# Inverting the chunk matrices of a linear recurrence on 32x32 blocks instead of 64x64

## The reference

```python
def _wkv7_step(state, inp):
    r_t, w_t, k_t, v_t, a_t, b_t = inp
    sa = jnp.einsum('bhvk,bhk->bhv', state, a_t)
    state = (state * w_t[:, :, None, :] + sa[..., None] * b_t[:, :, None, :]
             + v_t[..., None] * k_t[:, :, None, :])
    y = jnp.einsum('bhvk,bhk->bhv', state, r_t)
    return state, y
```

## Time and profile before

| | us |
|---|---|
| median of 3 runs (3816.68 to 3824.45) | 3817.28 |
| profiled execution, its own time | 3821.82 |
| span of the profile (first to last instruction) | 3820.0 |
| the chunk stage within it | 2341.4 to 2565.1 |

### The profile page before, as it was taken

The page is one execution under the profiler, slowest core; times in us unless marked ns, Lnnn a source line. Parts: engine busy times, 40 slices in busy tenths (PEclk is TensorE's granted clock), DMA queues, the critical chain, the costliest instruction groups (busy, mean ns, idle before and its releaser), DMA issues. The chain is left out here.

```text
span 3820.0 us, 58799 instructions
## 1 busy us (share of the span) xinstructions
PE 3543.2 (93%) x22333; PEld 2862.8 (75%) x22333; DVE 2333.9 (61%) x3638; ACT 1484.4 (39%) x2447; POOL 1348.4 (35%) x831
## 2 busy tenths in 40 slices
PE   8999998989988999899998998885999977889998
PEld 4787866779988999788886346873888854678887
DVE  5713176407998887788888665447566135755642
ACT  3212265325537994333332332222255203424540
POOL 3724300526784335442221001314344511413443
PEclk9999998999999999999999999997899987698999
DMA  7624401535678889999997243112233253033331
GB/s 281 218 91 135 144 36 74 190 107 186 223 234 299 320 321 381 354 366 361 355 352 256 75 138 111 59 42 98 70 94 99 100 143 75 1 127 84 88 121 55
DMA packets 372422, 655.35 MB, mean 172 GB/s; under 512 B 24152, under 2 KB 231896, under 8 KB 369028
## 3 DMA queue, kind: packets, MB, share of 16 engines
q1 hardware_dynamic: 324908, 477.04, 38.5%
q0 software_dynamic: 36864, 134.23, 9.4%
q10 hardware_dynamic: 10456, 41.40, 2.8%
HBM read 554.53 MB, written 98.06 MB: 171 GB/s over the span
## 5 line engine op out<-in xcount | busy, mean ns | idle before, releaser
L96 PE MATMUL ex_hb<-wb_x_hi,ex_uh 128*128 128x384 f32 x1024 | 350.9, 343 | 22.2 <-POOL ex_ul L1676 22.2
L2336 POOL TENSOR_TENSOR pf_wl<-pf_raw,pf_wh 128x2048 fp32r<-128x2048 f32 x48 | 221.3, 4611 | 395.2 <-ACT pf_wh L2283 395.2
L97 PE MATMUL ex_hb<-wb_x_lo,ex_uh 128*128 128x384 f32 x1024 | 344.9, 337 | 0.0
L98 PE MATMUL ex_hb<-wb_x_hi,ex_ul 128*128 128x384 f32 x1024 | 344.7, 337 | 0.0
L96 PE MATMUL es_ob<-es_vh,es_ah 128*128 128x512 f32 x768 | 300.3, 391 | 11.2 <-DVE es_al L2045 11.1
L96 PE MATMUL pf_acc<-wb_x_hi,pf_wh 128*128 128x512 f32 (+2 forms) x768 | 302.6, 394 | 4.7 <-DVE wb_x_lo L2378 4.7
L97 PE MATMUL pf_acc<-wb_x_lo,pf_wh 128*128 128x512 f32 (+2 forms) x768 | 302.1, 393 | 0.0
L98 PE MATMUL pf_acc<-wb_x_hi,pf_wl 128*128 128x512 f32 (+2 forms) x768 | 302.0, 393 | 0.0
L97 PE MATMUL es_ob<-es_vl,es_ah 128*128 128x512 f32 x768 | 299.9, 390 | 0.0
L98 PE MATMUL es_ob<-es_vh,es_al 128*128 128x512 f32 x768 | 299.7, 390 | 0.0
L2024 POOL DMA_INDIRECT es_near<-in_peer_v,wb_picked x128 | 165.9, 1296 | 338.2 <-DVE wb_po L2048 332.4
(11 more groups left out here) (520 smaller groups left out, 8939.7 us busy)
## 6 DMA issues: line engine op xcount, KB each, us to landing
ex_u<-in_uT SPq DMA_DIRECT2D x128, 512.0 KB
es_v<-in_peer_v SPq DMA_DIRECT2D x31, 2048.0 KB
pf_raw<-in_w_up SPq DMA_DIRECT2D x88, 512.0 KB, 5.2
ip_raw<-in_w_in SPq DMA_DIRECT2D x112, 256.0 KB, 4.3
scratch_act<-ex_ge SPq DMA_DIRECT2D x128, 192.0 KB
scratch_G<-eg_gates ACTq DMA_DIRECT2D x12, 2048.0 KB
es_ge<-scratch_act SPq DMA_DIRECT2D x31, 768.0 KB
es_g<-scratch_G SPq DMA_DIRECT2D x31, 768.0 KB
```

Of the source, the lines that this page charges most:

```text
L96: pe.matmul(out, left[0], right[0], start=start, stop=False)
L97: pe.matmul(out, left[0], right[1], start=False, stop=False)
L98: return pe.matmul(out, left[1], right[0], start=False, stop=stop)
L2336: pool.tensor_tensor(wl[:, u], raw[:, u], wh[:, u].bitcast(F32), ALU.subtract).then_inc(w_lo, 1)
```

## The change

- `LEVELS` is 4. The four levels work on 32x32 blocks alone: the tiles `em`, `ws`, `xx` have 32 columns instead of 64, and partition quarters 0 to 31, 32 to 63, 64 to 95, 96 to 127 hold the two diagonal blocks of both heads. `w_of` has 32 matmuls of 32x32 per unit and level, `d_of` has 64.
- The diagonal blocks are first copied together by four ScalarE activations per unit (`pick`, from `ba` to `ub`); GpSimd masks `ub`.
- `l_of` computes only diagonal blocks, with 32 matmuls instead of 16.
- The last level (joining 32 to 64) is a stage of its own for the one off-diagonal block: `last_w` 16 matmuls, `copy_last` (two ScalarE copies), `last_d` 16 matmuls, `corner` (two VectorE copies); `join` on GpSimd spreads the diagonal blocks into the 64x64 tile `xt`, which `az_of` reads.
- `copy_az` moves from VectorE to ScalarE. `copy_v`, `copy_k` and `mv_of` with its copy move to levels 0, 1 and 2.
- The masks loaded are `blocks` and `halves` instead of `lmask` and `emask`.

```diff
-    LEVELS = 5
+    LEVELS = 4
+    RB_ = RC // 2
+        em = sb("rc_em", [P, 2, LEVELS, NC_, RB_])
+        ub = sb("rc_ub", [P, 2, NC_, RB_])
+        xt = sb("rc_xt", [P, 2, NC_, 2, RB_])
+        quarters = [slice(RB_ * g, RB_ * g + RB_) for g in range(4)]
...
                         for c, p in TILES:
                             h, own = heads[c], tok[2 * i + p]
-                            mm = pe.matmul(pp[heads[p], u, 2 + c, i * RC:(i + 1) * RC], ar(s)[h, 0, own], bk(s)[h, 0, own],
-                                           start=True, stop=True)
+                            for j in range(2):
+                                block = slice(own.start + RB_ * j, own.start + RB_ * (j + 1))
+                                mm = pe.matmul(pp[quarters[2 * p + j], u, 2 + c, i * RB_:(i + 1) * RB_], ar(s)[h, 0, block],
+                                               bk(s)[h, 0, block], start=True, stop=True)
...
-                    for c, e in narrow:
-                        h = heads[c]
-                        mm = pe.matmul(one(u, 0)[h, e], em[h, u, lv, e, :], xx[h, u, 0, e, :], start=True, stop=True)
+                    for f in range(NC_):
+                        for g in quarters:
+                            mm = pe.matmul(low(u)[g, f], em[g, u, lv, f, :], xx[g, u, 0, f, :], start=True, stop=True)
...
+                    for f in range(NC_):
+                        for g in quarters:
+                            pe.matmul(pair(u)[g, 0, f], xx[g, u, 1, f, :], ws[g, u, f, :], start=True, stop=True)
+                        for g in quarters:
+                            mm = pe.matmul(pair(u)[g, 1, f], ws[g, u, f, :], xx[g, u, 1, f, :], start=True, stop=True)
...
+                def last_w(n):
+                    u = n % 2
+                    pe.wait_ge(x_added, nth(n, LEVELS - 1))
+                    for f in range(NC_):
+                        for p in range(2):
+                            g = quarters[2 * p]
+                            mm = pe.matmul(low(u)[quarters[2 * p + 1], f], ba[g, n % SLOTS, f, 0, RB_:RC], xx[g, u, 0, f, :],
+                                           start=True, stop=True)
...
+                def last_d(n):
+                    u = n % 2
+                    pe.wait_ge(last_w_copied, 2 * n + 2)
+                    for f in range(NC_):
+                        for p in range(2):
+                            g = quarters[2 * p + 1]
+                            mm = pe.matmul(pair(u)[quarters[2 * p], 1, f], ws[g, u, f, :], xx[g, u, 1, f, :],
+                                           start=True, stop=True)
...
+                    last_w(n)
+                    last_w(n + 1)
+                    last_d(n)
+                    last_d(n + 1)
                     az_of(n)
                     az_of(n + 1)
...
+                def corner(n):
+                    u = n % 2
+                    dve.wait_ge(last_d_done, n + 1)
+                    dve.wait_ge(joined, n + 1)
+                    for p in range(2):
+                        g = quarters[2 * p]
+                        dve.tensor_copy(xt[g, u, :, 1, :], pair(u)[g, 1]).then_inc(xt_full, 1)
...
+                def pick(n):
+                    act.wait_ge(ba_masked, n + 1)
+                    for g in range(4):
+                        act.activation(ub[quarters[g], n % 2], ba[quarters[g], n % SLOTS, :, 0, g % 2 * RB_:(g % 2 + 1) * RB_],
+                                       ACT.Copy).then_inc(picked, 1)
```

More of the change, by code:

```diff
@@ L2503, in _ @@
                         load(i + 1, u)
-                for to, name in zip(masks, ("mask2", "lmask", "emask", "eye2", "ident")):
+                for to, name in zip(masks, ("mask2", "blocks", "halves", "eye2", "ident")):
                     sp.dma_start(to[:], d[name]).then_inc(masks_loaded, 16)
@@ L2855, in d_of @@
                         pe.wait_ge(xt_ready, n + 1)
-                        pe.wait_ge(k_copied, n + 1)
-                        pe.wait_ge(v_copied, n + 1)
+                        pe.wait_ge(ab_copied, 2 * n + 2)
                     pe.wait_ge(w_copied, nth(n, lv))
[L2859 to L2869, removed]
@@ L2877, in mv_of @@
                         h = heads[c]
-                        mm = pe.matmul(one(u, 1)[h, e], ka[h, n % SLOTS, e, 0, :], rows[h, u, V_, e, :], start=True, stop=True)
+                        mm = pe.matmul(one(u, 2)[h, e], ka[h, n % SLOTS, e, 0, :], rows[h, u, V_, e, :], start=True, stop=True)
                     mm.then_inc(mv_done, 1)
@@ L2983, in add @@
                     dve.wait_ge(d_done, nth(n, lv))
[L2984 to L2994, removed]
+                    dve.tensor_tensor(xx[:, u], xx[:, u], pair(u), ALU.add).then_inc(x_added, 1)
+                def corner(n):
[5 more added lines that the diff above has]
+                        dve.tensor_copy(xt[g, u, :, 1, :], pair(u)[g, 1]).then_inc(xt_full, 1)
                 def add_r(n):
@@ L3025, in _ @@
                         add(n + 1, lv)
-                    copy_az(n)
-                    copy_az(n + 1)
+                    corner(n)
+                    corner(n + 1)
                     if n + 2 < KD:
@@ L3088, in _ @@
                         if lv == 0:
+                            copy_v(n)
+                            copy_v(n + 1)
+                        elif lv == 1:
+                            copy_k(n)
+                            copy_k(n + 1)
+                        elif lv == 2:
                             copy_mv(n)
                             copy_mv(n + 1)
+                    copy_last(n)
+                    copy_last(n + 1)
+                    copy_az(n)
+                    copy_az(n + 1)
+                    if n + 2 < KD:
+                        pick(n + 2)
                     copy_y(n)
+                    if n + 2 < KD:
+                        pick(n + 3)
                     copy_y(n + 1)
@@ L3759, in join @@
         return ((s // (2 * m) == t // (2 * m)) & (s // m < t // m)).astype(f)
-    c["lmask"] = np.stack([join(1, t, s), join(1, s, t)], 1)
-    c["emask"] = np.stack([join(m, s, t) for m in (2, 4, 8, 16, 32)], 1)
+    r, t = np.arange(P)[:, None] % (RC // 2), np.arange(RC // 2)[None]
+    c["blocks"] = np.stack([join(1, t, r), join(1, r, t), (r == t).astype(f)] + [join(m, r, t) for m in (2, 4, 8, 16)], 1)
+    first = (np.arange(P) % RC < RC // 2).astype(f)
+    c["halves"] = np.stack([first, 1 - first], 1)
     dist = np.maximum(T - 1 - np.arange(640), 0)
```

88 lines of the change are left out of this document (58 added, 30 removed).

## The result

The changed kernel takes 3903.28 us (median of 4 runs, 3898.56 to 3905.76); the kernel before took 3818.11 beside it (3816.68 to 3824.45). The ratio is 1.0219, with 95% interval 1.0203 to 1.0235. It is 2.2% slower.

What follows compares the result with a forecast made beforehand. Bound after the change: TensorE's program arriving, 256 instructions per 3.65 us. Stage 281.1 + 8 + 2.8 + 6.8 = 298.7 us, 75.0 over 223.7; 3821.8 + 75.0 = 3896.8, less 4.5 to the median: 3892, range 3860 to 3922.

Steps and rivals of the forecast that it cites:

- Number of pieces: TensorE's program in the stage: 19712 instructions after the change, 77 pieces of 256, against 51 before.
- Time per piece: TensorE's program in the stage: 256 instructions arrive in 3.65 us, all 77 in 281.1; a pair's level takes 11.0.
- Start: First 256 instructions of the stage: 2.8 us over a piece, because of the masks between them; stays.
- Loads: Three pieces of program disturbed by loads of the next units took 6.8 us more; this stays.
- What does not fit under a piece: `az_of` and the transposes: work exceeds the program's arrival by some 1 us, twice per pair, 8 us in all.
- Rival (b): Granted clock low through the levels: `az_of`, transposes and others take 36 us more at most, 3928; beyond 3920, chance 0.13.
- The price of a 32x32 matmul: Small matmuls in the levels: 14 ns per record, hidden under the program's arrival, term 0; at 28 ns about 0 to 10 us.
- Copies, additions, masks: Level work on ScalarE, VectorE and GpSimd: copy 0.39 us, addition 0.69, masks half of 1.31; hidden, saving nothing.
- Rival (a): Program no bound in the levels, smaller matmuls pay: 4.0 us per level, 40 us saved in all, 3777; chance 0.06.
- never shows: TensorE's instruction room, four times the others' (128 KB against 32 KB), was said never to show in the stage's 13056 instructions.

Runs made afterwards that it cites:

- the loop: Changed kernel with each pair's four levels as one loop on TensorE instead of written out, one mask buffer instead of four: 3811.5 us, ratio 0.9976 against the kernel before.

## Why the prediction came out right

The forecast was 3892 us and the median is 3903.28, within the range of 3860 to 3922, by the mechanism that was named. The forecast of the stage was 10.4 us too low, and so was that of the time (11.3). Its terms, one by one, for the stage of 309.1 us where 298.7 were expected:

- **Number of pieces.** 77 from the count of matmuls, 77 packets measured. Exact, and so is what the experiments removed: 77 - 36 = 41 in the loop, 77 - 24 = 53 with half the matmuls.
- **Time per piece.** From the resume at 2357.68 to that at 2379.80 lie six pieces in 22.12 us, 3.69 each, which is also the mean of all 42 single pieces without a load beside them; 3.65 was taken from four stretches before. 77 of them: 283.9 against 281.1. The level: 11.54 against 11.0.
- **Start.** The 2.8 us stayed nearly as they were: the first 128 matmul records now take 6.06 us. But the reason given, the masks between them, was wrong. TensorE did not wait there; it was busy from end to end at a low clock, as this stretch of the kernel before shows. The first 64 records of it took 3.69 us; the same 64 of a later pair, at a granted clock of 1.00, took 2.12.

```profile
2341.44:2347.78 6.34, 6.34 (x129) 6.20 (x133) 3.34 (x3) 0.00 (x0) 2.57 (x3) 0.55 0.94 311
```

- **Loads.** Three pieces beside loads took 6.21 + 5.90 + 6.66 us, a fourth 4.63; less 4 x 3.69 that is 8.6, against 6.8.
- **What does not fit under a piece.** The remainder, 309.1 - 283.9 - 2.8 - 8.6 = 13.8 us, against 8: the mis-sized term. `az_of` took 4.76 us for 62 records against 3.60, at a granted clock of 0.75, because it comes while the clock is still low. Over the four pairs it was busy for 21.9 us (first line, changed kernel) against 14.8 (second, before), and for 14.8 in the looped kernel too, where the levels run at the full clock:

```profile
L2917 PE MATMUL rc_pp<-rc_rhs,rc_xt 64*64 64x128 f32 x256 | 21.9, 349 | 0.3
...
L2887 PE MATMUL rc_pp<-rc_rhs,rc_xx 64*64 64x128 f32 x256 | 14.8, 271 | 0.0
```

  That is 7.1 us more, enough for the 5.8 missing. The remainder itself can be found in the trace: eight stretches of two to four pieces without a wait of over 0.5 us, most of them behind an inverse or at the start of a pair, took 91.5 us for 21 pieces, 14.0 more than 3.69 each. How the 14.0 divide between `az_of`, the transposes and the rest was not traced.

**Rival (b), the clock, was half right.** The clock did fall to 0.50, 1.2 GHz, in the levels, where TensorE stands nearly half of each piece. But it cost only what is in the last term, 5.8 us more than forecast and not the 36 of the rival: the work of a piece of 32x32 matmuls ends in under 2.5 us even so, as the stretches show, and the rest is waiting. The loop shows the reverse: where TensorE hardly stands, the granted clock is 1.00 (2369.5 to 2373.6 us, 3.73 us busy of 4.10).

**The price of a 32x32 matmul.** I took 14 ns and said that anything to 28 would not matter. At a clock of 0.50 it is (1.07 - 0.24) / 61 = 13.6 ns from the 62 records shown at 2365.17. In the loop at full clock 128 records of `w_of` took 1.44 us, some 10 ns each. The term was 0 as stated, since 128 records at 13.6 ns are 1.7 us. The 14 ns were read from a row at the full clock, so that they came true at half of it is luck; the bound of 28 ns is what carried the term.

**Copies, additions, masks.** Estimated from halves of known sizes; the groups of the stage:

```profile
L3164 POOL TENSOR_TENSOR rc_em<-rc_ub,rc_blocks 128x256 f32<-128x256 f32 x32 | 22.4, 728 | 313.0 <-ACT rc_ub L3078 313.0
L3020 DVE TENSOR_TENSOR rc_xx<-rc_xx,rc_pp 128x512 f32<-128x512 f32 x32 | 22.0, 688 | 172.9 <-PE rc_pp L2879 172.9
...
L3078 ACT ACTIVATE rc_ub<-rc_ba 32x256 f32<-32x256 f32 x32 | 13.3, 414 | 16.0 <-DVE rc_ba L2994 15.3
...
L3103 ACT ACTIVATE rc_ws<-rc_pp 128x256 f32<-128x256 f32 x32 | 12.3, 384 | 115.1 <-PE rc_pp L2866 115.1
...
L3085 ACT ACTIVATE rc_az<-rc_pp 128x1024 f32<-128x1024 f32 x8 | 8.2, 1024 | 23.7 <-PE rc_pp L2917 23.7
```

The copy was put at 0.39 us and takes 0.384, the addition at 0.69 and takes 0.688, `copy_az` at 1.04 and takes 1.02, a mask at half of 1.31 and takes 0.73, `pick` at up to 0.39 and takes 0.41. The additions, the copies of W and `copy_az` have idle time before them that TensorE ends. GpSimd waits for `pick` (270.8 of the 313.0 us are one wait, most of it ahead of the stage), and TensorE has no wait for a mask. Moving `copy_az` was put at 0, and two runs show 0.

**Rival (a)** needed pieces faster than 2.1 us. None shown came under 3.35. Its arithmetic of the matmuls was near, though: it gave 4.0 us for a level on TensorE, and the loop, which takes the program away as a bound, shows 4.09 and 4.27. Its 3777 us still don't come out of the loop, since the first turn and everything outside the levels (41 pieces, 151 us at 3.69) still come piece by piece. The Trainium skill ("TensorEngine Tiling (Array Packing)", Theoretical Speedup) gives up to four times for a dimension of at most 32, but also up to two for one of at most 64, which the kernel before already had. Looped, a level goes from 6.27 to 4.1 us, 1.5 times as fast; the runs agree in the direction, once the program is in place.

**One statement was wrong** without touching the sum: that TensorE's larger room "never shows". It was true of code that runs through once, and I read it as if it were true of TensorE. The loop's 768 instructions were fetched once, and no packet moved in its later turns. The trace of before had shown it outside the stage: in the experts' part, between 1215 and 1445 us, TensorE runs a loop of 640 matmuls and weight loads, a turn in 47.6 us. The DMA queues of that stretch:

```profile
q1 hardware_dynamic: 11155, 28.01, 36.8%
q0 software_dynamic: 6926, 25.21, 30.4%
q10 hardware_dynamic: 1440, 20.97, 22.3%
q14 instruction: 4, 0.03, 0.0%
```

There is no q8, the queue whose packets matched TensorE's pieces. Had I looked there, I would have had the remedy with the forecast. The Trainium skill ("Advanced Engine Details and Errata", ISA Cache) gives both two lines of 256 and 128 KB for TensorE. 768 instructions of 64 bytes are 48 KB: more than two lines hold, less than 128 KB. The trace agrees with the second figure and not with the first.

The rest of the span was assumed unchanged. In the profile it was 8.6 us shorter, so the stage's 85.4 us show as 76.8 in the spans; the medians differ by 85.2, which is the stage alone.

## What to carry to other kernels

Before small matmuls are packed more densely, count instructions: in an unrolled float32 stretch each matmul is four, 256 of them arrived in some 3.7 us here, and work that takes less than 14 ns per instruction (3.7 us over 256) is paid for at 14. "Issue" waits at equal instruction counts, with as many packets on the instruction queue, are the mark; the remedy is a loop round the dense part or fewer, wider matmuls, and large loads kept away from the stretches that still come piece by piece. Waits gathered ahead of such a loop have a price of their own (7.7 us here), and so has a change of tile shape between neighbouring matmuls (about 0.2 us here).

## What the runs showed of the hardware

- A loop of 768 TensorE instructions is fetched once and kept; its later turns take 4.1 to 4.3 us where unrolled levels take 11.5. What is the largest loop that stays wasn't tried.
- Code that runs through once gained no lead that lasts. Before the change the levels used a piece in 4.18 us (6.27 / 1.5), longer than one takes to come, and yet TensorE stood for a piece again behind them, for 1.18 us at 2507.04, with no transfer but the program's own packets in the 12 us before. A piece took 3.35 to 4.04 us undisturbed and up to 6.66 beside a load (6.75 before), although a packet lasts about 1.1 us. Where the other 2.6 us go, the profile doesn't show.
- A change between 64x64 and 64x32 tiles costs an estimated 0.18 to 0.24 us at a granted clock of 0.50; with 3584 changes the stage was 855 us longer and its granted clock 0.54 instead of 0.97.
- The granted clock was 0.50 there although TensorE's records left no gap (20.00 us busy of 20.00). In the unrolled levels of 32x32 it was 0.50 with TensorE busy for about half the time, and 1.00 in the same levels looped.
- A float32 matmul of one column with 64 new columns of weights costs 29 ns per record, as much as one of 64 columns.
- Half as many columns again on the same instructions raised the granted clock of the stage from 0.68 to 0.74 and changed its time by 0.2 us.
